# Cross attention in two pairs of heads: turning, scores and probabilities of a pair set between the steps of the query and output projections

## The reference, cut to what matters

```python
def cross_attn(xn, mem_k, mem_v, wq, wo, qn_g, kn_g):
    q = rmsnorm(split_heads(xn @ wq, XA_HEADS), qn_g)      # 4 heads of 256
    k = rmsnorm(mem_k, kn_g)                               # 256 memory rows
    s = jnp.einsum('bhsd,bhmd->bhsm', q, k).astype(jnp.float32) * (XA_HEAD_DIM ** -0.5)
    p = jax.nn.softmax(s, axis=-1).astype(xn.dtype)
    o = jnp.einsum('bhsm,bhmd->bhsd', p, mem_v)
    return (merge_heads(o) @ wo).astype(xn.dtype)
```

## Time and profile before

| | us |
|---|---|
| median of 3 runs | 1253.91 (1253.66 to 1254.07) |
| the profiled execution's own time | 1253.44 |
| its span, first to last instruction | 1251.7 |
| TensorE busy | 1172.5 (94%) |
| VectorE, ScalarE, GpSimd busy | 706.2, 587.5, 358.8 |
| attention of layer 0, first query step to last output step | 270.05 to 400.77 |
| attention of layer 1, likewise | 897.88 to 1029.1 |

### The profile page before, as it was taken

The page is one execution under the profiler, slowest core; times in us unless marked ns, Lnnn a source line. Parts: engine busy times, 40 slices in busy tenths (PEclk is TensorE's granted clock), DMA queues, the critical chain, the costliest instruction groups (busy, mean ns, idle before and its releaser), DMA issues.

```text
span 1251.7 us, 15333 instructions
## 1 busy us (share of the span) xinstructions
PE 1172.5 (94%) x5227; PEld 869.3 (69%) x5227; DVE 706.2 (56%) x1280; ACT 587.5 (47%) x1130; POOL 358.8 (29%) x311
## 2 busy tenths in 40 slices
PE   4999999999899799999899999979998997999996
PEld 2468876788667466666678877757887684666665
DVE  5893534320522688888744983771205216888887
ACT  2453246354723366665535364352546333566661
POOL 2024340564022021113136663253350220211120
PEclk9999999999999899999999999989998998999999
DMA  9433232376101799997232130022311008999963
GB/s 274 148 124 87 31 110 68 115 299 259 68 1 61 316 366 374 384 378 291 85 116 76 68 135 1 1 69 88 113 68 68 1 26 344 353 382 382 384 224 132
DMA packets 77643, 214.92 MB, mean 172 GB/s; under 512 B 23620, under 2 KB 24560, under 8 KB 65272
## 3 DMA queue, kind: packets, MB, share of 16 engines
q1 hardware_dynamic: 64688, 180.22, 39.1%
q0 software_dynamic: 10048, 28.92, 6.4%
q10 hardware_dynamic: 2840, 4.91, 1.1%
HBM read 187.90 MB, written 32.51 MB: 176 GB/s over the span
## 4 chain that ended last, share of the span: by engine, by line
PE 76%; DVE 13%; ACT 5%; issue 3%; DMA 1%; POOL 1%; DVEq 0%; POOLq 0%; ACTq 0%
PE bank L836 38%; PE bank L1166 7%; PE bank L1199 7%; PE bank L1171 6%; PE bank L1071 2%; PE bank L1112 2%; DMA E<-xs,idx 1%; DVE h L2321 1%; PE bank L1085 1%; PE bank L872 1%; PE bank L1015 1%; DVE E2r L2282 1%; PE bank L1222 1%; PE bank L1062 1%; PE bank L1340 1%
## 5 line engine op out<-in xcount | busy, mean ns | idle before, releaser
L675 POOL TENSOR_TENSOR wlo<-W,whi 128x512 fp32r<-128x512 f32 x176 | 254.5, 1458 | 469.8 <-ACT whi L1418 450.4
L1418 ACT ACTIVATE whi<-W 128x512 fp32r<-128x512 f32 x176 | 107.7, 633 | 245.5 <-PE bank L836 239.0
L836 PE MATMUL bank<-whi,xTr 128*128 128x512 f32 x480 | 192.2, 400 | 0.9 <-ACT E L1819 0.6
L836 PE MATMUL bank<-wlo,xTr 128*128 128x512 f32 x416 | 162.7, 391 | 0.0
L836 PEld LDWEIGHTS bank<-whi,xTr 128*128 128x128 f32 x480 | 90.7, 189 | 22.0 <-POOL wlo L675 1.7
L1171 PE MATMUL bank<-E4r,E1r 128*128 128x512 f32 x360 | 98.5, 422 | 0.0
L1199 PE MATMUL bank<-whi,E2r 128*128 128x512 f32 x256 | 90.5, 415 | 6.7 <-DVE E2r L2282 5.2
L1914 DVE TENSOR_TENSOR h<-bank,h 128x512 f32<-128x512 f32 x32 | 21.8, 692 | 131.3 <-PE bank L836 131.3
L836 PEld LDWEIGHTS bank<-wlo,xTr 128*128 128x128 f32 x416 | 78.7, 189 | 16.9 <-issue 1.2
L1171 PEld LDWEIGHTS bank<-E4r,E1r 128*128 128x128 f32 x360 | 67.5, 188 | 27.0 <-issue 7.4
L708 POOL COPY idx<-slots 128x1 uint32 (+1 forms) x30 | 5.5, 182 | 276.8 <-PE bank L1146 184.8
(11 more groups left out here) (485 smaller groups left out, 2433.5 us busy)
## 6 DMA issues: line engine op xcount, KB each, us to landing
E<-in_moe_w SPq DMA_DIRECT2D x48, 1024.0 KB, 10.2
W<-in_moe_w SPq DMA_DIRECT2D x32, 1024.0 KB, 9.8
xT<-in_moe_w SPq DMA_DIRECT2D x16, 1024.0 KB, 12.5
W<-in_od_w_in SPq DMA_DIRECT2D x7, 2048.0 KB, 8.7
ybuf<-E SPq DMA_DIRECT2D x26, 512.0 KB, 6.9
ybuf<-memV POOLq DMA_DIRECT2D x12, 1024.0 KB, 19.7
W<-in_w_mem_kv SPq DMA_DIRECT2D x4, 2048.0 KB, 8.5
W<-in_xa_wq SPq DMA_DIRECT2D x4, 2048.0 KB, 8.5
```

The lines of the kernel that those rows point to most:

```text
L675: pool.tensor_tensor(wlo[s_ % RING][:, :], slot(name)[:, k, :], whi[s_ % RING][:, :].bitcast(F32), ALU.subtract).then_inc(S["w_lo"], 1)
L836: ins = pe.matmul(bank(u + t)[:, :], a, b, start=(k == 0 and n == 0), stop=(k == KT - 1 and n == 2))
L1418: act.activation(whi[s_ % RING][:, :], slot(name)[:, k, :], ACT.Copy).then_inc(S["w_hi"], 1)
```

## The change

The four heads are treated as two pairs. A pair is one panel of the query projection.

TensorE now runs wq0; step 0 of wq1; 16 turnings of pair 0's queries; step 1; two score banks; step 2; two score banks; steps 3 and 4; 16 turnings of pair 0's probabilities; steps 5 to 7; the output of head 0; 16 turnings of pair 1's queries; the output of head 1; the four score banks of pair 1; steps 0 and 1 of wo0; 16 turnings of pair 1's probabilities; step 2; the outputs of heads 2 and 3; steps 3 to 7 of wo0; wo1.

ScalarE and VectorE follow in that order. Half of the scaled queries move from ScalarE to VectorE. The head norm is made once for each pair, on a strided view of 8 columns, so the root and the table for Exp come twice in a layer. The turned probabilities go to E5 instead of E4, the low parts of the head outputs to E4 instead of E1. All names of the attention keep their bank numbers from a common start ("in turn"), so pair 0 has one half of the banks and pair 1 the other. GpSimd's and SyncE's orders stay as they are.

```diff
-        return [(f"xa_norm{l}", 8), (f"q{l}", 8), (f"qT{l}", 8), (f"sc{l}", 8), (f"pT{l}", 8), (f"o{l}", 8),
-                (f"wo{l}", 8)]
+        return [(f"xa_norm{l}", 8)] + [(f"{name}{l}", 8, "in turn") for name in ("q", "qT", "sc", "pT", "o", "wo")]
...
-        pT = E[4][:, :].rearrange("p (h k q) -> p h k q", h=4, k=2)
+        pT = E5[:, 0:KT * T].rearrange("p (h k q) -> p h k q", h=4, k=2)
...
                 for n in range(2):
-                    split_gemm(first[f"wo{l}"] + 4 * n, f"wo{l}{n}", by_k(ohi), by_k(xlo["o"]), lambda k: taken(pe, first[f"o{l}"] + k))
+                    split_gemm(first[f"q{l}"] + 4 * n, f"wq{l}{n}", by_k(xhi), by_k(xlo["q"]),
+                               lambda k: taken(pe, first[f"xa_norm{l}"] + k),
+                               between={} if n == 0 else {0: [(turn_queries, 0)], 1: [(scores, 0), (scores, 1)],
+                                                          2: [(scores, 2), (scores, 3)], 4: [(turn_probs, 0)]})
+                head_out(0)
+                turn_queries(1)
+                head_out(1)
+                for t in range(TT):
+                    scores(TT + t)
+                for n in range(2):
+                    split_gemm(first[f"wo{l}"] + 4 * n, f"wo{l}{n}", by_k(ohi), by_k(xlo["o"]),
+                               lambda k: taken(pe, first[f"o{l}"] + k),
+                               between={} if n else {1: [(turn_probs, 1)], 2: [(head_out, 2), (head_out, 3)]})
...
+                queries(l, 0)
+                head_squares(l, 0, 0, 1)
+                weights(q1, RING, RING + 1)
+                turned(0)
+                head_squares(l, 0, 2, 3)
+                weights(q1, RING + 1, RING + 2)
+                head_root(0)
+                exps(0, 0)
+                exps(0, 1)
+                weights(q1, RING + 2, RING + 3)
+                exps(0, 2)
+                exps(0, 3)
+                weights(q1, RING + 3, KT)
+                weights(o0, 0, 1)
+                probs_turned(0)
+                weights(o0, 1, RING)
                 queries(l, 1)
...
+                out_high(0, 1)
+                head_squares(l, 1, 0)
+                out_high(1, 2)
+                head_squares(l, 1, 1)
+                turned(1)
+                head_squares(l, 1, 2)
+                out_high(2, 3)
+                head_squares(l, 1, 3)
+                out_high(3, 4)
+                head_root(1)
                 for t in range(TT):
...
+                    exps(1, t)
+                weights(o0, RING, RING + 2)
+                probs_turned(1)
+                weights(o0, RING + 2, RING + 3)
+                out_high(4, 8)
+                weights(o0, RING + 3, KT)
+                weights(f"wo{l}1", 0, RING)
                 weights_between(f"wo{l}1", None)
...
+                queries(0)
+                turned(0)
+                head_rstd(0)
+                for t in (0, 2):
+                    maxima(0, t)
+                    maxima(0, t + 1)
+                    normalise(0, t)
+                    normalise(0, t + 1)
+                probs_turned(0)
+                queries(1)
+                out_low(0, 2)
+                turned(1)
+                out_low(2, 4)
+                head_rstd(1)
+                maxima(1, 0)
+                for t in range(1, TT):
+                    maxima(1, t)
+                    normalise(1, t - 1)
+                normalise(1, TT - 1)
+                probs_turned(1)
+                out_low(4, 8)
                 add_to_h(f"wo{l}")
```

More of the change, by code:

```diff
@@ L1044, in attention @@
[L1044 to L1062, removed]
+                def turn_queries(half):
+                    for k in range(4 * half, 4 * half + 4):
+                        u = first[f"qT{l}"] + k
+                        claim(pe, u)
+                        for t in range(TT):
+                            if k % 4 == 0:
+                                taken(pe, first[f"q{l}"] + k + t)
+                            ins = pe.transpose(bank(u)[:, t * P:(t + 1) * P], qtok[:, t, k * P:(k + 1) * P], ident[:])
+                        fill(ins, u)
@@ new lines, in scores @@
+                def scores(n):
+                    hp, t = divmod(n, TT)
+                    u = first[f"sc{l}"] + n
+                    claim(pe, u)
+                    for head in range(2):
+                        for kk in range(2):
+                            k = 2 * (2 * hp + head) + kk
+                            if t == 0:
+                                taken(pe, first[f"qT{l}"] + k)
+                            ins = pe.matmul(bank(u)[:, head * NM:(head + 1) * NM], qT[:, k, t * P:(t + 1) * P],
+                                            memKT[:, k, :], start=(kk == 0), stop=(kk == 1))
+                    fill(ins, u)
@@ new lines, in turn_probs @@
+                def turn_probs(hp):
+                    for n in range(4):
+                        claim(pe, first[f"pT{l}"] + 4 * hp + n)
+                    for t in range(TT):
+                        pe.wait_ge(S["probs"], 8 * l + 4 * hp + t + 1)
+                        for n in range(4):
+                            u = first[f"pT{l}"] + 4 * hp + n
+                            ins = pe.transpose(bank(u)[:, t * P:(t + 1) * P],
+                                               prob[:, t, 2 * hp + n // 2, (n % 2) * P:(n % 2 + 1) * P], ident[:])
@@ L1625, in attention, with turned @@
[L1625 to L1628, removed]
+                def turned(half):
+                    for k in range(4 * half, 4 * half + 4, 2):
+                        u = first[f"qT{l}"] + k
+                        await_filled(act, u)
+                        evac(act.activation(qT[:, k, :], bank(u)[:, :], ACT.Copy, scale=g2[:, 2 * l:2 * l + 1]), u)
@@ new lines, in heads, with head_root, exps @@
+                def heads(ap, hp):
+                    return ap[:, 0:16].rearrange("p (t n) -> p t n", t=TT)[:, :, 2 * hp:2 * hp + 2]
+                def head_root(hp):
+                    act.wait_ge(S["hmean_ready"], (2, 6)[l] + hp)
+                    act.activation(heads(dstd, hp), heads(dsq, hp), ACT.Sqrt).then_inc(S["hstd_ready"], 1)
+                    table(ACT.Exp)
+                def exps(hp, t):
+                    u = first[f"sc{l}"] + 4 * hp + t
+                    act.wait_ge(S["max_ready"], (0, 24)[l] + 4 * hp + t + 1)
+                    for n in range(2):
+                        c = 4 * t + 2 * hp + n
+                        ins = act.activation(prob[:, t, 2 * hp + n, :], bank(u)[:, n * NM:(n + 1) * NM], ACT.Exp,
+                                             bias=xnm[:, c:c + 1], scale=drec[:, c:c + 1], accum_out=xsum[:, c:c + 1])
+                    evac(ins, u)
@@ L2099, in maxima, with queries @@
[L2099 to L2109, removed]
+                def queries(half):
+                    n = NORMS[f"xa_norm{l}"]
+                    for t in range(1, TT, 2):
+                        u = first[f"q{l}"] + 4 * half + t
+                        await_filled(dve, u)
+                        evac(ts(qtok[:, t, half * 512:(half + 1) * 512], bank(u)[:, :], rstd[:, n, t:t + 1], None, ALU.mult), u)
```

94 lines of the change are left out of this document (43 added, 51 removed).

## The result

| us | before | after |
|---|---|---|
| median of the runs | 1253.99 (4) | 1235.08 (4; 1233.99 to 1236.32) |
| span of the profiled execution | 1251.7 | 1232.2 |
| attention of layer 0 | 130.72 | 121.85 |
| attention of layer 1 | 131.26 | 121.84 |

After is faster: the ratio is 0.9844, 95% interval 0.9832 to 0.9856. Applied to the 1253.91 that stood before the forecast it is 1234.3, 19.6 us less; I had forecast 1237 and 16.6 us, in a range that began at 1234.9. The mechanism and the sign held, the size was too small by 2 to 3 us.

What follows compares the result with a forecast made beforehand. TensorE was taken to bound the kernel, losing attention time only to waits and a reduced clock. 17.5 us less 0.9 of net cost took 1253.44 to 1236.8; with 0.47 for the runs' median, 1237, range 1234.9 to 1243.

Steps and rivals of the forecast that it cites:

- What bounds: Attention: TensorE, busy 94%, loses time only to waits for first turnings and softmax and to turnings at a reduced clock.
- TensorE never waits: From wq0 to wo1, the new order was to leave no TensorE wait above 0.5 us.
- Its program: TensorE's pieces laid out on layer 0's clock, from wq0's end at 291.84 to wo1's end at 392.3.
- Rival 1: Pair 1's head norm and softmax late through two new table loads a layer: 1239, up to 1245; chance 0.16.
- my 1.7 us: Slack forecast for pair 1's last probabilities, ready at 345.0, before tile 3's turnings at 346.7.
- Rival 2: Waits of 1 to 2 us at each of four insertions in wq1, some 6 us a layer, near 1249; chance 0.06.
- Rival 3: TensorE's clock falls where f32 and split work alternate, 294.6 to 356.9; at 0.68, 1294; chance 0.03.
- The sum: Both attentions: 17.5 us given back less 0.9 us net cost, so 16.6 us won.
- The net cost of cuts: Six more changes to projection steps a layer at 0.09 us, against covered ends of runs: 0.9 us net.
- my own two terms: Cuts costing 1.1 us in all, against ends of matmul runs worth at most some 0.4 us a layer.
- The gross 17.5 us: Time lost between last query step and first head output: 8.5 us in layer 0, 9.0 in layer 1.
- The low end of my range: 1234.9: the whole 17.5 us won plus 0.5 us a layer for ends of runs now covered.

## Why the prediction was right in kind and too small in size

**What bounds, and that TensorE never waits**: right. Its program was met within 0.4 us at every piece, and a doubled piece costs its full length (3.50 us a layer).

**Rival 1, pair 1's chain late**: false. Slack was there, more than my 1.7 us, but I had the wrong event: turnings are released by the last bank's exponentials, since they claim its bank, and not by the last normalised tile. In the changed order both lie ahead of TensorE (342.73 and 343.57 against 345.14 and 346.45), so it did no harm; it did where I took the cover away. Of the price that the Trainium skill (page "ScalarE: Activation LUTs", section "What ACT_TABLE_LOAD costs") gives a table switch, a load of 1.28 us and 1.38 of draining, this kernel's rows show the load alone, also with four more switches in a row (loads 1.51 to 1.53 us apart, each with one activation of 0.20).

**Rival 2, new waits in wq1**: false; none at all. Even without VectorE's share it is 0.2 us a layer. **Rival 3, slower by a lower clock between two kinds of work**: false, 1.00 throughout. What the clock did follow in the attentions is long standing: 0.68 behind 4.4 us, 0.56 behind 3.9, and 1.00 where the same wait was filled. Behind the shorter waits, 1.0 us in the kernel before and 1.4 with pair 0 uncovered, it stayed at 1.00.

**The sum**: this step failed. 19.5 us of span went, against 16.6. Point by point:
- The net cost of cuts, 0.9 us, is nothing. I counted the longer first matmul behind a piece twice: 16 turnings with it, 1.66 + 0.09 = 1.75 us, are just half of the 3.49 us that 32 take alone and that the gross gain was worked out with, and then I took 0.09 us a change off again. Four more changes cost none that can be seen. And my own two terms, 1.1 us of cuts less 0.4 us a layer of ends, leave 0.3 and not the 0.9 that I took. 0.9 us.
- The gross 17.5 us for the two attentions measured 8.87 + 9.42 = 18.3. Score matmuls took 3.45 + 3.45 + 6.91 = 13.8 us where I put in 14.1, and the heads' outputs 3.43 + 3.44 + 6.87 = 13.7 against 13.97: pieces between other work have their end covered, which I had named as 0.4 us a layer and then set against the cuts. 0.8 us.
- 1.2 us lie outside the attentions. I had put them at nothing. The rank matmuls behind them took 9.53 and 9.40 us in this execution, 10.29 and 10.14 in that of before (granted clock in layer 0: 0.76 from 412.56 to 422.10, and 0.70 from 421.37 to 431.66), and one other piece, the 12 matmuls of one projection step at 834.36, took 4.01 against 4.60 at 843.47. These add to 2.1 us. Against them stands TensorE's wait for GpSimd ahead of that step, 1.8 us against 0.5; in the profiles of all versions, whose instructions are the same there, this wait is 0.5 or 0.6, 1.8 or 3.5 us. In the profiles of kernels that don't differ there, the 64 rank matmuls came out anywhere from 8.73 to 10.29 us, and in the kernel before with a filling 9.58 and 9.19, so two single executions can differ by this much for no reason of the change. That the change shifted nothing at all there isn't shown, and the cause of these 1.2 us stays open: by the runs' medians the whole is 18.9 and 19.2, by their ratios 19.6 and 20.0, with 18.3 accounted for.

The low end of my range took the whole 17.5 us and only 0.5 us a layer beyond it, which is what the attentions did (18.3); it had nothing for the differences between executions outside the change, which here are as large. In four of thirteen profiles another untouched stretch, 32 matmuls from 73.7, took 15.5 to 15.7 us and not 13.97, at a granted clock of 0.88 or 0.89 over 73.67 to 87.6 and not 1.00. Why the clock was lower in these four I don't know.

**Readings that did no harm**: the trace of before has two waits ahead of turned queries, 0.5 us together, and 1.0 us ahead of the scores behind VectorE's copy; I named only the first. A square costs 0.54 us by its starts, but not by the 4.04 / 8 that I gave for it, which is 0.51. VectorE's scaling of a tile took 0.75 us, where I took 0.7, and its normalising beside GpSimd was not longer (0.61 to 0.62). I had also said that the experts' stretches would be as long as before; the rank matmuls were not.

**Where the gain is**: 18.3 us in the attentions, of which 3.9 us the clock behind a wait, some 12 us waits and the rest ends of runs, all but VectorE's 0.4 by cover. Splitting without cover costs 10 us in the two attentions, and VectorE's half of the queries gives 0.4. The new bank numbers and buffers were in every version with pairs; what they do by themselves was not tested.

## What to carry to other kernels

Where one engine is busy 94% and its few waits have a clear owner, lay its program out piece by piece and ask for the slack at each; the gain is then the sum of waits and of what runs slowly behind them, and small pieces of other work between dense steps cost, here, just their own length. Splitting a dependent chain in two makes it longer and pays only as far as each half is covered: without cover it was slower than not splitting. A wait of 3.3 us or more cost more than itself here, since what came behind it ran at the lower clock; where such a wait can't be covered, work that nobody reads is a cheap stand-in. Two single profiles say little about stretches that a change doesn't touch: the same instructions took 13.97 us in one execution and 15.67 in another.

## What the runs showed that I had not expected

- The clock's share. A wait of 3.3 to 4.4 us was followed by turnings at one and a half times to twice their length (16 in 3.1 to 3.6 us for 1.75, 32 in 5.35 and 5.91 for 3.49), and sometimes by a slow projection step (3.14 for 2.73). In one place of the routing, once in each layer, 56 turnings without a reader made the kernel 4.6 to 4.9 us faster.
- A bank claimed ahead of its first use binds work to the last reader of the bank. With pair 0 uncovered, tile 0's probabilities were normalised by 303.2, and their turning stood until 307.6 for the exponentials of tile 3.
- VectorE's scaling of 128x8 numbers, 0.17 us elsewhere, took 0.93 us where GpSimd was splitting weights, in both layers at the same place. It began at 300.65 and ended 0.03 us behind GpSimd's instruction; I did not test what holds it.

```profile
300.29 1.26 POOL L674 TENSOR_TENSOR wlo<-W,whi 128x512 fp32r<-128x512 f32 x1 [2.54 <-ACT whi L1435]
...
300.65 0.93 DVE L2168 TENSOR_SCALAR st<-st 128x8 f32<-128x8 f32 x1
```
